# Building a half product stage's weight sums six pieces later, and storing the last token tile in quarters

## What is computed

```python
h = rmsnorm(x, norm_w)
proj = h @ w_in                      # 2048 x 7184, columns split:
gq, gk, gv, gg, glr, hq, hf, hi, hg = split(proj)
log_a = log_sigmoid(glr @ gla_w_up + gla_b_up) / 16
o_a = gated_linear_attention(gq, gk, gv, log_a)      # 4 heads, values 256 wide
o_b = gated_linear_attention(hq, 1 - f, hi, log(f))  # 8 heads, f from hf
mixed = concat(head_rmsnorm(o_a) * silu(gg), head_rmsnorm(o_b) * silu(hg))
out = rmsnorm(x + mixed @ w_out, final_norm_w)
```

## Time and profile before

| what | value |
|---|---|
| median of 3 runs | 895.16 us (893.78 to 895.2) |
| the profiled execution | 893.98 us, its span 892.2 us |
| PE busy | 878.4 us, 98% of the span |
| mean granted clock of PE | 0.998 |
| DVE, ACT busy | 602.0 us (67%), 412.7 us (46%) |
| DMA moved | 167.64 MB, mean 188 GB/s |

### The profile page before, as it was taken

One profiled execution on the slowest core, in us unless ns is written; L12 is line 12 of the kernel. 1 busy time (PEld: TensorE's weight loads), 2 busy tenths in 40 slices (PEclk: granted clock), 3 DMA queues, 4 the chain that ended last, 5 costly groups with the idle time before them and its releaser, 6 DMA issues.

```text
span 892.2 us, 11634 instructions
## 1 busy us (share of the span) xinstructions
PE 878.4 (98%) x4323; PEld 730.9 (82%) x4323; DVE 602.0 (67%) x982; ACT 412.7 (46%) x554; POOL 83.8 (9%) x125
## 2 busy tenths in 40 slices
PE   8999999999999999999999999999999999999996
PEld 5786888888888888888888888888888888888885
DVE  6624377743587737487887878888884769556757
ACT  6521442324444325173464554745654455335544
POOL 3010111110000101011110100100111110000000
PEclk9999999999999999999999999999999999999999
DMA  7286569988755746567765654445776988865654
GB/s 271 71 279 215 165 191 228 201 192 250 223 182 151 244 144 210 166 167 153 161 146 139 144 178 142 148 138 173 155 145 147 258 206 272 298 205 190 198 179 189
DMA packets 75164, 167.64 MB, mean 188 GB/s; under 512 B 7333, under 2 KB 15561, under 8 KB 73961
## 3 DMA queue, kind: packets, MB, share of 16 engines
q1 hardware_dynamic: 45266, 108.02, 36.2%
q0 software_dynamic: 16896, 50.34, 26.2%
q10 hardware_dynamic: 12952, 8.61, 3.4%
HBM read 158.56 MB, written 58.72 MB: 244 GB/s over the span
## 4 chain that ended last, share of the span: by engine, by line
PE 89%; DVE 4%; DMA 3%; ACT 2%; issue 1%; ACTq 0%; DVEq 0%
PE main L551 54%; PE main L798 8%; PE main L739 5%; PE sc L798 4%; PE sc L605 4%; DMA raw<-in_w_in 3%; PE st L798 2%; PE po L798 2%; PE sc L597 2%; PE po L632 2%; PE sc L739 1%; DVE w_lo L1229 1%; PE po L635 1%; PE st L617 1%; ACT w_hi L840 1%
## 5 line engine op out<-in xcount | busy, mean ns | idle before, releaser
L551 PE MATMUL main<-h_hi,w_hi 128*128 128x512 f32 x640 | 261.1, 408 | 0.1
L551 PE MATMUL main<-h_hi,w_lo 128*128 128x512 f32 x640 | 250.3, 391 | 0.0
L551 PE MATMUL main<-h_lo,w_hi 128*128 128x512 f32 x640 | 249.7, 390 | 0.0
L1229 DVE TENSOR_TENSOR w_lo<-raw,w_hi 128x1024 fp32r<-128x1024 f32 x102 | 124.6, 1222 | 120.2 <-ACT w_hi L840 119.4
L840 ACT ACTIVATE w_hi<-raw 128x1024 fp32r<-128x1024 f32 x102 | 107.7, 1057 | 206.0 <-PE main L551 166.1
L551 PEld LDWEIGHTS main<-h_hi,w_lo 128*128 128x128 f32 x640 | 120.1, 188 | 26.8
L551 PEld LDWEIGHTS main<-h_lo,w_hi 128*128 128x128 f32 x640 | 120.6, 188 | 21.9
L551 PEld LDWEIGHTS main<-h_hi,w_hi 128*128 128x128 f32 x640 | 120.5, 188 | 21.8 <-issue 0.5
L861 ACT ACTIVATE ex<-ex 128x512 f32<-128x512 f32 (+2 forms) x84 | 52.0, 640 | 60.8 <-DVE ex L1359 48.0
L551 PE MATMUL main<-w_hi,h_hi 128*128 128x512 f32 x128 | 50.6, 395 | 1.0 <-DVE val L1471 0.6
L1688 DVE TENSOR_TENSOR w_lo<-feat,w_hi 128x1024 fp32r<-128x1024 f32 x26 | 31.8, 1224 | 28.1 <-ACT w_hi L1153 27.9
(11 more groups left out here) (302 smaller groups left out, 1524.8 us busy)
## 6 DMA issues: line engine op xcount, KB each, us to landing
raw<-in_w_in SPq DMA_DIRECT2D x104, 512.0 KB, 4.6
w_sum<-in_w_out POOLq DMA_DIRECT2D x48, 512.0 KB, 5.0
w_sum<-in_w_in POOLq DMA_DIRECT2D x24, 512.0 KB, 6.1
w_sum<-w_sum POOLq DMA_DIRECT2D x24, 512.0 KB, 5.2
raw<-w_sum SPq DMA_DIRECT2D x24, 512.0 KB, 4.1
feat<-w_sum SPq DMA_DIRECT2D x24, 512.0 KB, 4.2
raw<-in_w_out SPq DMA_DIRECT2D x14, 512.0 KB, 4.4
feat<-in_x SPq DMA_DIRECT2D x6, 1024.0 KB, 7.4
```

Source lines behind the costliest of these rows:

```text
L551: mm = pe.matmul(main[c][:, :], a, b, start=(k == 0 and j == 0), stop=(k == KT - 1 and j == 2))
L1229: dve.tensor_tensor(w_lo[:, q % SPL, :, :], raw[:, q % RAW, :, :], w_hi[:, q % SPL, :, :], ALU.subtract).then_inc(lo_ok, 1)
```

## The change

The pacing of the first 32 POOL transfers starts at count 7 (`NP - 1`) in place of 1. The adding transfers of this stage come in the order X1, X2, X4, X3 in place of X1, X3, X2, X4. For token tile 1 ACT's scaling is two instructions of 512 columns, DVE signals after each of its two, and SyncE stores four quarters of 256 KB in place of two halves of 512 KB.

```diff
@@ sync
-            for j, t in enumerate((2, 3, 0, 1)):
+            def store(t, cols):
+                sp.dma_start(out[t * P:(t + 1) * P, cols], y[t][:, cols]).then_inc(out_done, 16)
+
+            for j, t in enumerate((2, 3, 0)):
                 sp.wait_ge(yn, j + 1)
-                sp.dma_start(out[t * P:(t + 1) * P, D // 2:], y[t][:, D // 2:]).then_inc(out_done, 16)
+                store(t, slice(D // 2, D))
                 sp.wait_ge(y_left, j + 1)
-                sp.dma_start(out[t * P:(t + 1) * P, 0:D // 2], y[t][:, 0:D // 2]).then_inc(out_done, 16)
-            sp.wait_ge(out_done, 2 * 16 * NT)
+                store(t, slice(0, D // 2))
+            for n in range(2):
+                sp.wait_ge(yn, 4 + n)
+                store(1, slice(D // 2 + n * GW, D // 2 + (n + 1) * GW))
+                sp.wait_ge(y_left, 4 + n)
+                store(1, slice(n * GW, (n + 1) * GW))
+            sp.wait_ge(out_done, 2 * 16 * NT + 32)
@@ gpsimd
-            paced = [1]
+            paced = [NP - 1]
...
-                for j, (name, source) in enumerate(ADDED):
+                for name, source in ([ADDED[i] for i in (0, 2, 3, 1)] if pair == 2 else ADDED):
+                    j = XS.index(name)
                     pool.wait_ge(w_copied[pair * len(XS) + j], 16 * QP)
@@ scalar
                     act.wait_ge(y_fn, j + 1)
-                    act.activation(y[t][:, p0], y[t][:, p0], ACT.Copy,
-                                   scale=rs[:, 4 * t + 2:4 * t + 3]).then_inc(y_left, 1)
+                    for cols in (slice(0, GW), slice(GW, 2 * GW)) if t == 1 else (p0,):
+                        act.activation(y[t][:, cols], y[t][:, cols], ACT.Copy,
+                                       scale=rs[:, 4 * t + 2:4 * t + 3]).then_inc(y_left, 1)
@@ vector
                     if t < 2:
-                        dve.tensor_scalar(y[t][:, pq], y_w[:, t, :], by, None, ALU.mult)
+                        mm = dve.tensor_scalar(y[t][:, pq], y_w[:, t, :], by, None, ALU.mult)
+                        if t == 1:
+                            mm.then_inc(yn, 1)
```

## The result

| | before | after |
|---|---|---|
| median | 893.9 us (18 runs, 893.23 to 896.84) | 898.02 us (18 runs, 895.96 to 900.81) |
| the profiled execution | 893.98 us, span 892.2 | 899.02 us, span 897.2 |

The ratio is 1.0046, with a 95% interval of 1.0037 to 1.0055: slower by 4.1 us in the medians, by 5.0 us in the profiled executions. The median of before is 1.3 us under the 895.16 of the three runs that the forecast was put on. The runs after are spread over 4.9 us; only three of the 18 before are over 895.2.

The account below looks back on a forecast made before the run. PE, busy 98% of the span, was taken as the bound. On the profiled execution 893.98 - 0.6 + 5.5 - 0.2 = 898.7 us, put on the median 899.9; the range was 893.6 to 904.5.

Parts of the forecast that it names:

- Where PE can gain: Group 1, near 69 us: later POOL copies let loads and a weight split come earlier, removing PE's bank-copy wait; -0.6 us.
- DMA work against the time to piece 11: Half product stage, from 208.45 us: 32.1 us of adds and loads in 25.0 us, short by 7.1; term +5.5 us.
- How it comes about: Half product stage: PE waits for `w_lo` between product pieces 8 and 13, 3.6 to 7.1 us in all.
- the adds starving the loads: Rival, half product stage: adds go strictly first, PE waits from piece 5, costing 11.6 us; 906.0 us, chance 0.06.
- a load does not overtake an add in flight: DMA queues: a load issued at 205.16 moved only 0.01 MB up to 207.4 while the add had 94.4%.
- The measure of lead: Half product stage: DMA short by 7.1 us up to piece 11, the splits' three pieces of lead already counted.
- X3 and X4 in time: Half product stage: both finish before SyncE needs them, X4 for product piece 16 and X3 for piece 20; term 0.
- The quarters: Last token tile's scaling and stores: stream begins 0.39 us earlier, shorter rows cost 0.2; term -0.2 us, ends -0.4 and +0.3.
- The rival with room on the DMA engines: Half product stage: measured shares are partly waiting packets, several adds overlap and nothing is lost; 894.4 us, chance 0.27.
- The base: Whole kernel: 898.7 us from the profiled execution, put on the runs' median of 895.16 as 899.9 us.

Follow-up runs that it names:

- plain copies: The full change with the eight adds of X4 and X3 made copies of the same bytes at the same counts: 893.48 us against 894.2 before, ratio 0.9986.
- start 7 and order: The kernel before with only POOL's start at count 7 and the new order of adds, old two stores: 897.57 us against 894.4, ratio 1.0052.

## Why the prediction was right, and where it was not

- **Where PE can gain: the path right, the -0.6 not shown.** The wait at group 1 went and the stage starts 0.54 us earlier, and the split was through at 65.3, forecast near 65.5. But the term was read from one profile in which that wait stood. With the old start and the quarters it didn't stand, and two profiles without it have a wait of 0.6 us near 295 us in its place. The term lies between 0 and -0.6.
- **DMA work against the time to piece 11: right in sign and size.** +5.5 was forecast for the stage, 5.9 measured in the profile, and in the medians 4.1 plus what the two gains gave, 4.1 to 4.8 (4.1 + 0.6 + 0.1). The plain copies show that the adding is the cause, and that an add takes twice the DMA time of a copy. The DMA share was above 1 from 208 to 240 us and 0.71 from 240 to 245, where the forecast had it above 0.95 until about 245.
- **How it comes about: wrong in three things.**
  1. The forecast put the waits at pieces 8 to 13; they came before 5 and 7. Piece 5 was my own mark for the adds starving the loads; the place was that rival's, the price (11.6 us there) was not, since loads kept getting turns. I had let transfers go whole, in turn or by arrival, and piece 5's load landed at 221.2, beside nearly three adds. The step "a load does not overtake an add in flight" rests on little: the load of the earlier trace rows was issued at 205.16, and a load issued at 224.20 with no add about had its packets from 225.1 on, so it stood still for some 1 us, not for 3. With both queues full the packets alternate, and loads with 2 KB rows get 0.45 MB in 5 us. Even that doesn't give the 10.6 us of piece 5's load, in which its queue moved 1.01 MB; this rest stays open. The sum also looked at piece 11 alone, and no earlier piece was put to the same test.
  2. The loss was to be all waiting. It was 3.35 us of waiting and 1.75 us of a lower clock, which no term had. The waits, forecast at 3.6 to 7.1 us in all, were too few for the loss and the clock made it up. That the two errors offset each other is luck.
  3. The work was summed as if shares added up to 1. They reach 1.08. If that is work done side by side, the engines do some 8% more than I counted, of 32 us of work 2.5 us; no run tells this apart from packets that wait longer.
- **The measure of lead.** The sum took the lateness as growing with the work. The starts don't bear that out: about 1 us in the medians at 3 (not told from nothing by the ratio), nothing at 5, 2.4 us by the ratio at 6, 4.1 at 7. A step between 5 and 6 is seen, a rule for its place isn't.
- **X3 and X4 in time: right.** SyncE issued the load of piece 20 at 252.86, far behind X3's last add of 228.50, and PE had no wait at pieces 12 to 20. The order itself buys nothing that was seen.
- **The quarters: right that it is little.** Forecast -0.2, profile -0.2, runs 0.9996 (0.9988 to 1.0005), which doesn't tell it from nothing.
- **The rival with room on the DMA engines** was half right for a smaller dose: with five adds in the stage no loss was measured, though one of two profiles had 1.8 us of waits.
- **The base.** The forecast of 899.9 stood on a median that was 1.3 us high. Put on 893.9 it is 898.6, against 898.02.

## What to carry to other kernels

A background transfer that is moved away from one busy place lands in another: count the DMA time per step of the new place (here 2.8 to 3.5 us of adds and 1.4 us of load in each 2.72 us) before moving it, and give it a deadline as well as a start. Packing the cheap copies closer kept the later start without the loss. A wait of 0.6 us in one profile need not be there in the next: before it is booked as a gain, look whether it stands in a second execution, and whether an engine behind it would be ready earlier too. Where a loss depends on which queue is served first, one profile may be a mild or a bad execution: read the cause in it, and take the size from the runs.

## What the hardware showed that I had not expected

- With one add in flight a load's packets stood still until it was through, for some 1 us of the 3 in the earlier trace rows. With both queues full they came one for one (210 to 222 and 198 to 200 packets), with 4 KB beside 2 KB and with 2 KB on both sides, so the side with larger rows got more bytes.
- A load can land long after its queue has moved its bytes' worth: 10.6 us and 1.01 MB for the 0.52 MB of piece 5 in the change, 5.1 us and 0.58 MB in the mild execution of start 7 and order.
- An add between places in HBM took 2.7 us of DMA time for 0.52 MB in the stage, a plain copy of the same bytes 1.3 us.
- After PE waits of 2.38 and 2.50 us the granted clock went to its lower level some 0.8 us after the restart, for 3.8 and 3.4 us. After waits of 0.78 to 0.98 us in six other executions it stayed up.
- The shares of the queues sum to 1.03 to 1.10 where both are full: a share near 1 there isn't a fixed amount of work.
